# Two copies by ScalarE and an add by GpSimd for one copy and an add by VectorE, in the attentions of a hybrid block

## What is computed

```python
def dense_gqa_attention(q, k, v):            # 8 heads of 64, 2 key/value heads
    def block(qi):
        sc = jnp.einsum('bqkgd,bskd->bkgqs', qi, k).astype(jnp.float32) * scale
        p = jax.nn.softmax(sc, axis=-1).astype(v.dtype)
        return jnp.einsum('bkgqs,bskd->bqkgd', p, v)
...
def mla_attention(q_lat, q_rope, c_kv, k_rope, w_uv):      # 8 heads, latent keys and values
        sc = (jnp.einsum('bqhc,bsc->bhqs', ql, c_kv)
              + jnp.einsum('bqhr,bsr->bhqs', qr, k_rope)).astype(jnp.float32) * scale
        p = jax.nn.softmax(sc, axis=-1).astype(c_kv.dtype)
...
    oa = oa * jax.nn.silu(ga)
    ob = mla_attention(q_lat, q_rope, ckv, k_rope, w_uv) * jax.nn.silu(gb)
    return jnp.concatenate([oa, ob], axis=-1) @ w_out
```

## Time and profile before

| | |
|---|---|
| median of 3 runs | 3069.89 us (3068.4 to 3070.27) |
| the profiled execution | 3071.16 us, span 3069.3 us |
| PE (TensorE matmul) | 2921.9 us busy, 95% |
| PEld (weight load) | 2444.4 us, 80% |
| DVE (VectorE) | 1703.1 us, 55% |
| ACT (ScalarE) | 1253.8 us, 41% |
| POOL (GpSimd) | 385.7 us, 13% |

### The profile page before, as it was taken

One profiled execution on the slowest core, in us unless ns is written; L12 is line 12 of the kernel. 1 busy time (PEld: TensorE's weight loads), 2 busy tenths in 40 slices (PEclk: granted clock), 3 DMA queues, 4 the chain that ended last, 5 costly groups with the idle time before them and its releaser, 6 DMA issues.

```text
span 3069.3 us, 38258 instructions
## 1 busy us (share of the span) xinstructions
PE 2921.9 (95%) x15282; PEld 2444.4 (80%) x15282; DVE 1703.1 (55%) x2162; ACT 1253.8 (41%) x2084; POOL 385.7 (13%) x224
## 2 busy tenths in 40 slices
PE   8999998899999999999999999889999899999998
PEld 6877886687888777888888777778888778879986
DVE  6554576663544444443444745688888745316664
ACT  5321456332433111111112335577767624427751
POOL 0000005100000000000000000255544300004420
PEclk9999999999999999999999999999999999999999
DMA  4112335032222223232321222100001231131031
GB/s 143 55 41 61 119 104 185 28 110 83 83 69 81 70 74 87 87 89 75 89 81 52 83 79 62 56 1 6 14 18 35 97 106 45 55 93 44 17 110 70
DMA packets 226590, 219.35 MB, mean 71 GB/s; under 512 B 9456, under 2 KB 195056, under 8 KB 224880
## 3 DMA queue, kind: packets, MB, share of 16 engines
q1 hardware_dynamic: 221664, 200.07, 21.0%
q10 hardware_dynamic: 4752, 16.84, 1.5%
HBM read 180.12 MB, written 34.67 MB: 70 GB/s over the span
## 4 chain that ended last, share of the span: by engine, by line
PE 85%; DVE 6%; ACT 3%; issue 2%; POOL 2%; DMA 1%; SPq 0%; ACTq 0%; DVEq 0%; POOLq 0%
PE P L342 60%; PE P L280 5%; PE P L2408 3%; PE P L311 2%; PE P L283 2%; PE P L285 2%; PE P L284 2%; POOL T L2668 1%; PE P L2422 1%; PE P L1104 1%; PE P L2421 1%; DVE PTL L1517 1%; DVE WST L2647 1%; ACT wh L259 1%; PE P L1552 1%
## 5 line engine op out<-in xcount | busy, mean ns | idle before, releaser
L267 DVE TENSOR_TENSOR wl<-wf,wh 128x1024 fp32r<-128x1024 f32 (+4 forms) x239 | 251.6, 1053 | 943.3 <-ACT wh L259 943.0
L259 ACT ACTIVATE wh<-wf 128x1024 fp32r<-128x1024 f32 (+4 forms) x239 | 219.8, 920 | 1097.4 <-PE P L342 998.3
L342 PE MATMUL P<-AQ,wh 128*128 128x512 f32 x1824 | 490.6, 391 | 8.7 <-issue 7.3
L2668 POOL TENSOR_TENSOR T<-T,WST 128x1024 f32<-128x1024 f32 x128 | 242.4, 1894 | 1619.6 <-DVE WST L2640 1619.6
L342 PEld LDWEIGHTS P<-AQ,wh 128*128 128x128 f32 x1824 | 342.2, 188 | 81.4 <-issue 9.2
L342 PE MATMUL P<-XH,wh 128*128 128x512 f32 (+1 forms) x1264 | 396.2, 395 | 9.6 <-DVE XL L1346 5.2
L342 PE MATMUL P<-XL,wh 128*128 128x512 f32 (+1 forms) x1264 | 391.3, 391 | 0.0
L342 PE MATMUL P<-XH,wl 128*128 128x512 f32 (+1 forms) x1264 | 391.0, 391 | 0.0
L342 PEld LDWEIGHTS P<-XH,wh 128*128 128x128 f32 (+1 forms) x1264 | 235.5, 187 | 66.4 <-issue 15.4
L342 PE MATMUL P<-AQ,wl 128*128 128x512 f32 x912 | 281.4, 390 | 0.0
L342 PEld LDWEIGHTS P<-XL,wh 128*128 128x128 f32 (+1 forms) x1264 | 236.3, 187 | 52.5
(11 more groups left out here) (436 smaller groups left out, 5082.9 us busy)
## 6 DMA issues: line engine op xcount, KB each, us to landing
AW<-ada_w SPq DMA_DIRECT2D x48, 512.0 KB, 3.7
wf<-w_gate_up SPq DMA_DIRECT2D x44, 512.0 KB, 4.9
H<-scratch_h SPq DMA_DIRECT2D x32, 512.0 KB, 6.8
wf<-w_in SPq DMA_DIRECT2D x28, 512.0 KB, 3.8
scratch_h<-H SPq DMA_DIRECT2D x24, 512.0 KB, 5.7
scratch_g<-T ACTq DMA_DIRECT2D x22, 512.0 KB, 3.0
wf<-odd_w_in SPq DMA_DIRECT2D x20, 512.0 KB, 3.7
wf<-even_w_in SPq DMA_DIRECT2D x17, 512.0 KB, 3.8
```

The lines of the kernel that those rows point to most:

```text
L259: e.activation(self.sb["wh"][i % 2][:, 0:m], self.sb["wf"][i % 2][:, 0:m], ACT.Copy).then_inc(*self.s.w_hi.up(i))
L267: e.tensor_tensor(l, f, h.bitcast(F32), ALU.subtract).then_inc(*self.s.w_lo.up(i))
L342: ins = e.matmul(self.P[slot][0:m, t:t1], w, x[:, k, t:t1], start=first and k == 0, stop=last and k == kb - 1)
L2668: e.tensor_tensor(self.px(n), self.px(n), r, ALU.mult).then_inc(*s.pool.up(("sc", n)))
```

## The change

In an even step ScalarE copies both halves out of PSUM: rows 0 to 63 straight into their place in O, rows 64 to 127 into TOK. GpSimd adds TOK to O in SBUF, after its scaling of block n. GpSimd's two operands stand in the same rows, so TOK's half is chosen by the half of O, which is the same for four outputs in a row (`half`), and ScalarE waits for GpSimd's add of the output before. GpSimd waits for what it has issued itself (`here`) ahead of each of its instructions. TensorE's banks are free after ScalarE's second copy. The gates wait for GpSimd's adds, and ScalarE waits for the second rope's end before output 48.

```diff
--- before.py
+++ after.py
@@ -2347,8 +2347,10 @@
         h = p // 4 % 8
         return self.sb["O"][64 * (h % 2):64 * (h % 2) + 64, 4 * (p // 32) + h // 2, 256 * (p % 4):256 * (p % 4) + 256]
 
-    def half(self, u):
-        return self.sb["TOK"][64 * u:64 * u + 64, 0:256]
+    def half(self, p):
+
+        a = 64 * (p // 4 % 2)
+        return self.sb["TOK"][a:a + 64, 0:256]
 
     def pv(self, u):
         return self.P[3][:, 512 * u:512 * u + 512]
@@ -2424,7 +2426,7 @@
                     e.matmul(o[0:64, :], v[:, k, 0:64], PL[:, k, :], start=False, stop=False, skip_group_check=True)
             if part:
                 ins.then_inc(*s.mm.up(("pv", n // 2)))
-                free[u] = [(s.dve, ("o", n // 2))]
+                free[u] = [(s.act, ("half", n // 2))]
 
         def slab(name, g):
             i = self.no[name, g]
@@ -2488,7 +2490,7 @@
             if 0 <= at < 128:
                 values(at, part)
         self.emptied = {0: [(s.act, ("exp", 126))], 1: [(s.act, ("exp", 127))], 2: [(s.lo, ("pt", 127, 1))],
-                        3: [(s.dve, ("o", 63))]}
+                        3: [(s.act, ("half", 63))]}
 
     def pair_free(self, h):
 
@@ -2561,11 +2563,14 @@
                     self.act_weights(e, self.no[i])
             if n % 2 == 0 and 0 <= n - 5 < 128:
                 p = (n - 5) // 2
-                u = p % 2
+                o = self.pv(p % 2)
                 e.wait_ge(*s.mm.to(("pv", p)))
-                if p > 1:
-                    e.wait_ge(*s.dve.to(("o", p - 2)))
-                e.activation(self.half(u), self.pv(u)[64:128, 0:256], ACT.Copy).then_inc(*s.act.up(("half", p)))
+                if p:
+                    e.wait_ge(*s.pool.to(("o", p - 1)))
+                if p == 48:
+                    e.wait_ge(*s.lo.to(("rope end", 1)))
+                e.activation(self.result(p), o[0:64, 0:256], ACT.Copy).then_inc(*s.act.up())
+                e.activation(self.half(p), o[64:128, 0:256], ACT.Copy).then_inc(*s.act.up(("half", p)))
 
 
     WEIGHTS = {("rv", 1): 57, ("qk", 1): 88, ("eo", 0): 92, ("eo", 1): 121}
@@ -2652,24 +2657,28 @@
             for i, position in self.WEIGHTS.items():
                 if position == n:
                     self.dve_weights(e, self.no[i])
+
+    def pool_attention(self, e):
+
+        s = self.s
+        for n in range(134):
+            if n < 128:
+                w = self.sb["WST"][n % 4]
+                e.wait_ge(*s.act.to(("exp", n)))
+                e.wait_ge(*s.dve.to(("inv", n)))
+                e.wait_ge(*s.pool.here())
+                e.tensor_tensor(self.px(n), self.px(n), w[:, 2:3].to_broadcast([128, 1024]),
+                                ALU.mult).then_inc(*s.pool.up(("sc", n)))
             if n % 2 == 0 and 0 <= n - 5 < 128:
                 p = (n - 5) // 2
                 e.wait_ge(*s.act.to(("half", p)))
-                e.tensor_tensor(self.result(p), self.pv(p % 2)[0:64, 0:256], self.half(p % 2),
-                                ALU.add).then_inc(*s.dve.up(("o", p)))
-
-    def pool_attention(self, e):
-
-        s = self.s
-        for n in range(128):
-            r = self.sb["WST"][n % 4][:, 2:3].to_broadcast([128, 1024])
-            e.wait_ge(*s.act.to(("exp", n)))
-            e.wait_ge(*s.dve.to(("inv", n)))
-            e.tensor_tensor(self.px(n), self.px(n), r, ALU.mult).then_inc(*s.pool.up(("sc", n)))
+                e.wait_ge(*s.pool.here())
+                e.tensor_tensor(self.result(p), self.result(p), self.half(p), ALU.add).then_inc(*s.pool.up(("o", p)))
 
     def dve_gate(self, e, j):
         O = self.sb["O"][:, j, :]
         e.wait_ge(*self.s.act.to(("gate", j)))
+        e.wait_ge(*self.s.pool.to(("o", 8 * j + 7)))
         e.tensor_tensor(O, O, self.sb["GA"][:, j, :], ALU.mult).then_inc(*self.s.dve.up(("gate", j)))
 
     def sp_attention(self, e):
```

## The result

Before and after were timed on the same chip. Before took 3069.14 us (median of 4, 3067.59 to 3070.27), after 3090.31 us (median of 4, 3088.68 to 3091.31). The ratio is 1.0064, with a 95% interval of 1.0051 to 1.0077: slower by 21 us by the medians, by 16 to 24 us by the interval, where 19.6 was forecast. The spans of the profiled executions are 3069.3 and 3089.5 us; those executions took 3071.16 and 3091.31 us.

What follows compares the result with a forecast made beforehand. First half bound by a chain through GpSimd, second by PE. The new ring of 6.85 us a pair with odd-step jobs adds 16.2, the second half 3.4: 19.6 on 3069.9 gives 3089 us, range 3076 to 3104.

Steps and rivals of the forecast that it cites:

- The ring: First half: ScalarE's copy waits for GpSimd's add of the previous output, a loop of 6.85 us a pair against 6.54.
- Which price of the add: GpSimd's 64x256 add: 0.73 us by the rate for two full operands, 0.62 by the broadcast rate; bounds 0.62 to 0.84.
- The jobs of odd steps: First half: VectorE's further jobs between maximum and reciprocal lengthen the loop, 0.61 us per short job, 16.1 in all.
- PE's wait on GpSimd in the first half: First half: PE's waiting for GpSimd was to grow from 19 to 35 us.
- The second half: Last 64 blocks: +3.4 us in sum, from 2.4 in seven heads, +2.0 in the last, less about 1 gained.
- Seven heads: Second half: two k pairs put the loop behind, 0.34 us reaches PE, q pairs catch up; 2.4 us for seven heads.
- The sign named for the k pairs: Second half: pairs whose job is k were to grow from 7.10 us by 0 and then 0.3.
- The last head: End of second half, without such jobs: four pairs go from 26.42 to 28.4 us, +2.0.
- The gain at the second rope end: Second half: PE waited 3.2 us for VectorE's add; ScalarE now frees that bank about 1 us earlier.
- rival 4: First half: PE's clock falls to its lower level in a tenth of it, +13 us more, 3102; chance 0.08.
- Rival 1: First half: old chain without the add decides, 29 pairs from 6.54 to 5.98, -16 us, total 3053; chance 0.05.
- the chain: First half before: dependencies through GpSimd, ScalarE and VectorE repeating every 6.54 us a pair; 5.98 without VectorE's add.

Runs made afterwards that it cites:

- both remedies: Changed kernel with a second place for the upper half's copy and GpSimd's add ahead of the scaling of block n: 3063.53 us, ratio 0.9978 to before.

## Why the prediction was right

The direction, the mechanism and the size of the ring held. That the sum came within 2 us of the measured time is in part luck, as the terms show one by one:

- **The ring.** Forecast 6.85, measured 6.91 in plain pairs. The add took 0.72 for 0.73, GpSimd to ScalarE 0.10 (0.82 less 0.72) for 0.10, the copies 0.80. The one term that was off is from the scaling to the add behind it: 2.04 for 1.94. GpSimd waits there for its own semaphore, and the handover took the upper bound, 0.15. The two experiments that open the ring in different ways both bring the pair below the old one, and shortening the add by 0.41 shortens it by 0.41.
- **Which price of the add.** Of the two rates in the earlier trace rows the one with two full operands was right. By form, after: instruction, count, busy and mean ns, idle before it.

```profile
L2676 POOL TENSOR_TENSOR O<-O,TOK 64x256 f32<-64x256 f32 x64 | 47.1, 736 | 15.2 <-ACT TOK L2573 6.3
```

 The Trainium skill (GPSIMD Engine Reference, 4.1 Engine selection) has GpSimd about two times slower than VectorE at this. The trace shows 0.736 against VectorE's 0.42, 1.75 times, where VectorE took one of its operands from PSUM. The rule's advice holds against this edit by its result, but not for its reason: with the add ahead of the scaling the slower engine does it in a kernel faster than before.
- **The jobs of odd steps.** Pairs with a short job took 7.51 where 7.46 was forecast, and the move into even steps gave 6.92. All jobs together were 16.1 of the 214.8 forecast for 29 pairs, 198.6 before. By the same cut, from the first to the thirtieth output (ScalarE's second copies), after takes 218.5, so the half was forecast 3.7 too short. Cut at PE's scores of blocks 6 and 64, which is 29 pairs as well, it went from 199.0 to 217.3, +18.3; 29 times the 0.06 of the ring is 1.7 of the 2.1 that the forecast fell short. The +17.0 of the table comes out nearer only because the stretch ahead of block 6 took 17.8 before and 16.4 after: before had its clock low there for 6.8 us and after had not, and the other kernels whose clock was not low there took 16.4 to 16.5 too.
- **PE's wait on GpSimd in the first half.** Forecast to grow from 19 to 35; by the same cut it grew from 20.5 to 30.8. That step was off by its assumption that the whole loss shows as idle time of PE. Of the 17.0 us, 12.1 are idle time (24.2 before, 36.3 after, from the length and the busy time of the windows) and 4.9 are busy time for the same matmuls (192.6 to 197.5). The clock averaged 0.98 in both: it was low for 10.2 us in each, with PE busy for 9.1 and 9.2 of them, so it is not the clock. Matmul ends are modelled in the profile, and no run here parts that 4.9; it stays open.
- **The second half.** The sum held, +3.5 up to the last score and 0.7 from there to the projection for +3.4, but two of its three terms did not (all by PE's scores). Seven heads were to lose 0.34 each, 2.4 in all. Blocks 64 to 92, ahead of the second rope's end, lost 0.1 together: their pairs with v and rope jobs, of 7.8 to 9.2, are longer than the ring even before. The three heads behind it lost 1.05: two of them take 30.22 each where they took 29.78, +0.44. The ring with its job is 7.50, forecast 7.46, and three of four outputs there are 7.50 apart. The sign named for the k pairs did not come out: they stay at 7.11 and 7.13, and the q pair behind them takes 8.19 for 7.80. The last head lost 1.4 up to the last score and 0.7 behind it, 2.1 for 2.0; its outputs came to 8.25 and three times 6.91, 29.0, forecast 28.4. And the second rope's end, which was to gain 1.0, lost 1.0. That the two misses cancel is luck.
- **The gain at the second rope end.** It came, and a longer stretch of low clock took more than it gave. PE's wait for the bank fell from 3.2 to 2.0, by about the 1 us forecast. The row of PE's waits in the second half of after, and two windows of after around the end of that wait:

```profile
PE P L283 <- ACT TOK L2573: 2.0, 1, 2.0
```

```profile
2299.00:2303.50 4.50, 2.55 (x14) 1.70 (x13) 3.38 (x5) 3.68 (x7) 0.07 (x1) 1.00 0.07 16
2303.50:2310.50 7.00, 6.10 (x24) 4.88 (x23) 4.65 (x8) 3.90 (x8) 4.44 (x3) 0.53 0.12 28
```

 PE idled for 1.95 before 2302.50 at full clock; from about 2303.8 it was granted about half of it, the level of 1.2 GHz, for nearly 7 us. Six score matmuls took 2.91 there, and 1.64 at 2.4 GHz; the pair took 10.39 for 9.22 before. In before the clock fell behind PE's idle time too, but for 3.4 us: 0.53 from 2287 to 2290, then 0.92 over the next four us.

 The other kernels free the bank as after does. From the score of block 92 to that of block 96, around this end, the add-first kernel, the short add and both remedies had no low clock and took 19.1; two places, with 3.4 us of it, took 19.7 to 19.8 in three profiles and 19.1 in the one without; the two copies without an add and the jobs in even steps, with 6.8 us, took 21.5, as after did. Before, with 3.4 us, took 20.5. So the freed bank is worth 0.7 at equal clock, and the low stretch cost 0.7 when it was short and 2.4 when it was long. That is rival 4's mechanism, at one place. In the first half it did not grow: the clock was low for 10.2 us in before and after alike.
- **Rival 1's price was wrong**, though its case didn't arise. It set the gain of a plain pair (0.56, measured 0.58) on 29 pairs and got -16. The kernels without a ring gained 7. 13 of the 29 pairs are plain; they gave 6.8, since three of them had been at 6.29 and not 6.54. The 16 others and the first steps gave nothing in sum in the kernel with two copies and no add (216.8 to 210.1 for the half); those with v and rope kept their length (6.56 and 6.86), since PE's own work with the job's matmuls was already about level with the chain. Had the ring not decided, the forecast would have been 9 us too fast. The step that fails is "29 pairs from about 6.54 down to 5.98": the prediction had PE's 5.66 for a plain pair and never worked it out for a pair with a job.

## What to carry to other kernels

A buffer with one place between two engines closes a ring through everything that stands between its release and its next use, in both engines' queues and in those that they feed. Add up that ring before the loads of the engines: here 6.91 against 5.96 cost 28 us, though no engine in it was busy for three quarters of the time. A second place gave 23 of them back, the consumer's instruction put earlier in its queue 27. When a chain is shortened, count the gain only over those repetitions in which the chain is what comes last, and work out the next bound for each kind of repetition separately. And check a forecast term by term: here the second half came out nearly right, though two of its three terms were off by more than 1 us each.

## What the runs showed of the hardware beyond the forecast

The prediction weighed a rule of the Trainium skill (SBUF - State Buffer, Who interferes with whom), by which a VectorE instruction with two SBUF inputs and a GpSimd one that reads SBUF shut each other out. In the trace of before no row showed it. After has two places where a gate on VectorE, whose two inputs lie in SBUF, meets an add on GpSimd (timeline, both engines):

```profile
2447.32 1.22 DVE L2682 TENSOR_TENSOR O<-O,GA 128x1024 f32<-128x1024 f32 x1 [1.68 <-ACT GA L2537]
2448.16 0.96 POOL L2676 TENSOR_TENSOR O<-O,TOK 64x256 f32<-64x256 f32 x1 [4.48 <-ACT TOK L2573]
2449.20 2.36 DVE L2682 TENSOR_TENSOR O<-O,GA 128x1024 f32<-128x1024 f32 x2 [0.66 <-ACT GA L2537]
2450.99 1.15 POOL L2676 TENSOR_TENSOR O<-O,TOK 64x256 f32<-64x256 f32 x1 [1.87 <-ACT TOK L2573]
```

The adds began at different points of the gates and took 0.96 and 1.15 where the other 62 take about 0.73, but both end 0.58 after the gate beside them: 2448.16 + 0.96 = 2449.12 against 2447.32 + 1.22 = 2448.54, and 2452.14 against 2451.56. In the kernel with the add of 64 columns the same two take 0.55 and 0.75 for 0.32 and end 0.18 to 0.19 after theirs:

```profile
2430.28 1.23 DVE L2682 TENSOR_TENSOR O<-O,GA 128x1024 f32<-128x1024 f32 x1 [1.68 <-ACT GA L2537]
2431.14 0.55 POOL L2676 TENSOR_TENSOR O<-O,TOK 64x64 f32<-64x64 f32 x1 [4.90 <-ACT TOK L2573]
```

That fits an add that does its 256 or 64 columns only once VectorE's instruction is through, and a gate that is not lengthened (1.22 to 1.23 in all). The same two meetings stand in the other kernels with the full add, with 0.95 to 0.96 and 1.15 for it.

The other way round it is VectorE that waits. With the jobs in even steps an add starts just ahead of the first rope's last sum, whose two inputs lie in SBUF too:

```profile
2072.53 0.72 POOL L2676 TENSOR_TENSOR O<-O,TOK 64x256 f32<-64x256 f32 x1
2072.59 1.75 DVE L2612 TENSOR_TENSOR T<-T,O 128x1024 f32<-128x1024 f32 x1
```

The add keeps its length, and VectorE's sum takes 1.75, where it takes 1.22 in every other kernel and at the second rope's end of this one. So by this case's rows the rule holds, and whichever of the two starts second pays, 0.2 to 0.5 us in each such meeting; for VectorE that is read from this one. At the end of the attention it does not lie on the path of after: the chain of work that ended last goes there from ScalarE's copies and its work on the gates to the last gate and the projection, not through the adds. GpSimd's recorded ends are rough: the last gate, which waits for the last add, starts 0.11 before that add's recorded end. No kernel was made to vary this alone.
